# Sixteen of the thirty position bias thresholds as 0/1 tiles times a table on TensorE

## The reference, cut to what matters

```python
def _rel_bucket(rel):
    nb = REL_BUCKETS // 2
    max_exact = nb // 2
    n = jnp.abs(rel)
    large = max_exact + (jnp.log(jnp.maximum(n, 1).astype(jnp.float32) / max_exact)
                         / math.log(REL_MAX_DIST / max_exact) * (nb - max_exact)).astype(jnp.int32)
    large = jnp.minimum(large, nb - 1)
    return jnp.where(rel > 0, nb, 0) + jnp.where(n < max_exact, n, large)
...
        bucket = _rel_bucket(positions[:, None, :] - qpos[:, :, None])
        bias = jnp.moveaxis(rel_bias[bucket], -1, 1).astype(jnp.float32)
        s = jnp.where(key_chunk[None, :] <= qc[:, None], s + bias[:, :, None], -jnp.inf)
```

## Time and profile before

| | us |
|---|---|
| median of 3 runs | 2300.75 |
| lowest, highest | 2299.51, 2301.26 |
| the profiled execution | 2304.66 |
| its span in the profile | 2302.5 |
| PE busy in it | 2190.8 (95%) |
| DVE busy | 1599.7 (69%) |
| ACT busy | 1183.7 (51%) |

### The profile page before, as it was taken

One profiled execution on the slowest core, in us unless ns is written; L12 is line 12 of the kernel. 1 busy time (PEld: TensorE's weight loads), 2 busy tenths in 40 slices (PEclk: granted clock), 3 DMA queues, 4 the chain that ended last, 5 costly groups with the idle time before them and its releaser, 6 DMA issues.

```text
span 2302.5 us, 39325 instructions
## 1 busy us (share of the span) xinstructions
PE 2190.8 (95%) x17010; PEld 2056.2 (89%) x17010; DVE 1599.7 (69%) x2015; ACT 1183.7 (51%) x1405; POOL 0.2 (0%) x4
## 2 busy tenths in 40 slices
PE   6977999999899999999998999799999999998997
PEld 6856888888799999999998999799999999998997
DVE  8986899998696678446556665696676445657663
ACT  3534477777553554434854444353654436744442
POOL 0000000000000000000000000000000000000000
PEclk8978799999999999999999999899999999999999
DMA  8544399999544544444333444254544444344552
GB/s 343 193 172 150 149 374 373 371 369 364 201 166 161 184 151 166 147 147 149 109 134 140 165 173 173 112 182 148 186 165 165 152 159 148 110 150 144 186 189 83
DMA packets 64316, 432.06 MB, mean 188 GB/s; under 512 B 7792, under 2 KB 11152, under 8 KB 13712
## 3 DMA queue, kind: packets, MB, share of 16 engines
q1 hardware_dynamic: 64144, 429.56, 51.1%
HBM read 428.45 MB, written 1.08 MB: 187 GB/s over the span
## 4 chain that ended last, share of the span: by engine, by line
PE 88%; DVE 7%; ACT 2%; issue 1%; DMA 1%; SPq 0%; ACTq 0%; DVEq 0%
PE banks L1823 63%; PE banks L1841 10%; PE quad L1841 5%; DVE area_y L2295 1%; PE quad L552 1%; PE single L565 1%; DMA spare<-in_units_first 1%; PE quad L516 1%; PE quad L452 1%; DVE slot_rounded L998 1%; PE quad L555 1%; PE quad L500 1%; PE quad L540 1%; ACT area_y_rounded L650 0%; PE quad L472 0%
## 5 line engine op out<-in xcount | busy, mean ns | idle before, releaser
L1823 PE MATMUL banks<-spare_rounded,slot_rounded 128*128 128x272 f32 (+1 forms) x2176 | 624.8, 287 | 0.0
L1823 PE MATMUL banks<-spare_rounded,area_y_rounded 128*128 128x272 f32 (+1 forms) x1504 | 439.1, 292 | 15.1 <-DVE hn_rounded L987 13.1
L1823 PE MATMUL banks<-area_x_rounded,slot_rounded 128*128 128x272 f32 (+1 forms) x1568 | 447.0, 285 | 0.0
L1823 PE MATMUL banks<-hn_rounded,area_y_rounded 128*128 128x272 f32 (+1 forms) x1504 | 432.1, 287 | 0.0
L1823 PEld LDWEIGHTS banks<-spare_rounded,slot_rounded 128*128 128x128 f32 x2176 | 413.2, 190 | 0.0
L998 DVE TENSOR_TENSOR slot_rounded<-slot,area_y_rounded 128x2048 fp32r<-128x2048 f32 x118 | 269.6, 2289 | 161.2 <-ACT area_y_rounded L650 161.1
L1823 PEld LDWEIGHTS banks<-spare_rounded,area_y_rounded 128*128 128x128 f32 x1504 | 286.5, 190 | 17.5 <-DVE hn_rounded L987 14.0
L1823 PEld LDWEIGHTS banks<-area_x_rounded,slot_rounded 128*128 128x128 f32 x1568 | 297.2, 190 | 0.0
L1823 PEld LDWEIGHTS banks<-hn_rounded,area_y_rounded 128*128 128x128 f32 x1504 | 286.1, 190 | 0.1
L650 ACT ACTIVATE area_y_rounded<-slot 128x2048 fp32r<-128x2048 f32 x118 | 223.7, 1906 | 32.8 <-PE banks L1823 32.8
L998 DVE TENSOR_TENSOR slot_rounded<-slot,area_x_rounded 128x2048 fp32r<-128x2048 f32 x52 | 119.0, 2292 | 93.2 <-ACT area_x_rounded L650 93.1
(11 more groups left out here) (544 smaller groups left out, 5102.2 us busy)
## 6 DMA issues: line engine op xcount, KB each, us to landing
slot<-in_units_second SPq DMA_DIRECT2D x236, 1024.0 KB, 4.8
slot<-in_units_moe SPq DMA_DIRECT2D x100, 1024.0 KB, 5.1
slot<-in_units_first SPq DMA_DIRECT2D x32, 1024.0 KB, 5.6
spare<-in_units_moe SPq DMA_DIRECT2D x20, 1024.0 KB, 5.0
spare<-in_units_first SPq DMA_DIRECT2D x6, 1024.0 KB, 5.3
slot<-in_units_second SPq DMA_DIRECT2D x8, 768.0 KB, 4.2
merged<-acs_rows SPq DMA_DIRECT2D x4, 544.0 KB, 5.2
slot<-in_units_first SPq DMA_DIRECT2D x2, 576.0 KB, 4.0
```

The lines of the kernel that those rows point to most:

```text
L1823: ins = nc.tensor.matmul(out, weights[w], x[a], start=start and i == 0, stop=stop and i == 2, **kw)
```

## The change

The fourteen lowest thresholds stay as they were. For the other sixteen the distance of 256 keys to a query is compared on another layout: partition p = 16 g + r holds threshold r for the eight groups g of keys. `bias_key` is key position minus threshold, for 16 keys of each group of the first query block (128 keys) and 32 of the second's (256 keys), 48 in all. `reach_keys(part)` writes, for 16 of these, a tile [128, 16 keys, 128 queries] of ones where the key minus the threshold is at or above the query's position. `bias_table` [128, 32] holds in row p the four heads' steps of threshold r, in the four columns of group g, and zeros elsewhere. PE multiplies each [128, 128] tile with the table (48 matmuls of 32 columns in three parts of 16), which sums the thresholds and gives 128 queries by 8 groups by 4 heads. The three parts go to banks of `quad` at 1536, 0 and 512: the bank of x's mean square and those of the first two modulation pairs. They stand behind every second early unit. `bias_products` adds the results to `bias`. The mask addition moves from before the modulation pairs to before `weights_low(8)`.

The position input grows by 48 and the parameter input by 65 columns.

```diff
+BIAS_DIRECT = 14
+BIAS_GROUPS, BIAS_ROWS = 8, len(BUCKET_STARTS) - BIAS_DIRECT
+BIAS_KEYS = SCORES // BIAS_GROUPS
+BIAS_WIDTH = BIAS_GROUPS * DIFF_HEADS
...
+BIAS_BANKS = (1536, 0, 512)
...
     tick(ins, s.x_stat)
-    for u in ADA_EARLY:
+
+    def bias_keys(part):
+
+        pe.wait_ge(s.bias_reached.sem, s.bias_reached.at(0, part + 1))
+        if part == 0:
+            pe.wait_ge(s.x_root.sem, 1)
+        else:
+            pe.wait_ge(s.h1_ready.sem, part)
+        for n in range(16):
+            at = BIAS_BANKS[part] + BIAS_WIDTH * n
+            nc.tensor.matmul(m.quad[:, at:at + BIAS_WIDTH], m.bias_reach[:, 16 * part + n, :], m.bias_table, start=True, stop=True, skip_group_check=True)
+
+    for n, u in enumerate(ADA_EARLY):
         ada_rows(u)
+        if n % 2 and n < 6:
+            bias_keys(n // 2)
...
     link(copy(m.pos[:, :], m.pos_int[:, :]))
+    tick(tt(m.bias_table, p1("bias_of", 0, BIAS_WIDTH), p1("bias_before", 0, BIAS_WIDTH), ALU.subtract), s.dve1_step)
+    tick(ts(m.bias_key, m.pos[:, 2 + SEQ:], p1("bias_start"), None, ALU.subtract), s.dve1_step)
...
-    steps = list(range(len(BUCKET_STARTS)))
+    steps = list(range(BIAS_DIRECT))
+
+    def reach_keys(part):
+
+        keys, queries = slice(16 * part, 16 * part + 16), 2 + (128 if part else 0)
+        tick(tt(m.bias_reach[:, keys, :], m.bias_key[:, keys].unsqueeze(2).to_broadcast([128, 16, 128]),
+                m.pos[:, queries:queries + 128].unsqueeze(1).to_broadcast([128, 16, 128]), ALU.is_ge), s.bias_reached)
+
+    def bias_products():
+
+        for part, at in enumerate(BIAS_BANKS):
+            a, n, first_key = (0, 128, 0) if part == 0 else (128, 256, 16 * part - 16)
+            out = m.bias[:, :, a:a + n].rearrange("p h (g n) -> p h g n", g=BIAS_GROUPS)[:, :, :, first_key:first_key + 16]
+            products = m.quad[:, at:at + 512].rearrange("p (n g h) -> p h g n", g=BIAS_GROUPS, h=DIFF_HEADS)
+            tick(tt(out, products, out, ALU.add), s.dve1_step)
...
-    settle()
-    bias_steps(1)
-    v.wait_ge(m.loaded_early.sem, 16)
-    settle()
-    tick(tt(m.bias, m.bias, m.chunks.unsqueeze(1).to_broadcast([128, DIFF_HEADS, SCORES]), ALU.add), s.dve1_step)
+    for part in range(2):
+        reach_keys(part)
...
-        if pair < 2:
+        if pair == 0:
+            reach_keys(2)
+        elif pair == 1:
             bias_steps(1)
...
     weights_low(2)
-    bias_steps(2)
+    settle()
+    bias_products()
+    settle()
+    bias_steps(1)
     weights_low(3)
...
     normalise_rows(0, m.dq_tok)
     bias_steps(2)
+    settle()
+    tick(tt(m.bias, m.bias, m.chunks.unsqueeze(1).to_broadcast([128, DIFF_HEADS, SCORES]), ALU.add), s.dve1_step)
     weights_low(8)
...
     normalise_rows(2, m.q_tok)
-    bias_steps(1)
     root = roots(3)
...
             root.rearrange("p (b h) -> p b h", b=2).unsqueeze(3).to_broadcast([128, 2, MLA_HEADS, MLA_ROPE]), ALU.mult), s.rows_normed)
-    bias_steps(3)
     read_ada(8)
...
         normalise(i)
         if i in ADA_PAIR_BEHIND:
             read_ada(ADA_PAIR_BEHIND[i])
-        if i < 7:
-            bias_steps(2 if i in (2, 5) else 1)
-            settle()
```

More of the change, by code:

```diff
@@ L1393 @@
                  (6, 22), (7, 23), (8, 24), (12, 25), (16, 26), (23, 27), (32, 28), (46, 29), (64, 30), (91, 31)]
+BIAS_DIRECT = 14
+BIAS_GROUPS, BIAS_ROWS = 8, len(BUCKET_STARTS) - BIAS_DIRECT
+BIAS_KEYS = SCORES // BIAS_GROUPS
+BIAS_WIDTH = BIAS_GROUPS * DIFF_HEADS
+assert BIAS_GROUPS * BIAS_ROWS == 128
+BIAS_BANKS = (1536, 0, 512)
 TWO_PI = (6.28125, 0.0019350051879882812, 3.0199159819e-07)
@@ L1398 @@
                ("dq_g", 1), ("dk_g", 1), ("lambdas", 4), ("subln", 1), ("rel_bias", BUCKETS * DIFF_HEADS),
-               ("b_router", ROUTER), ("w_router", KT * ROUTER), ("c", KT), ("q_rope", MLA_ROPE), ("k_rope", MLA_ROPE), ("inv_freq", MLA_ROPE // 2)]
+               ("b_router", ROUTER), ("w_router", KT * ROUTER), ("c", KT), ("bias_start", 1), ("bias_of", BIAS_WIDTH), ("bias_before", BIAS_WIDTH), ("q_rope", MLA_ROPE), ("k_rope", MLA_ROPE), ("inv_freq", MLA_ROPE // 2)]
 PAR1_AT, PAR1 = {}, 0
@@ L2617, in first_signals @@
     s.lambda_products = Signal(sem("first_lambda_products"))
+    s.bias_reached = Signal(s.lambda_products.sem, 0, 1)
     s.lambda_sums = Signal(sem("first_lambda_sums"))
@@ L2789, in program @@
         a = Area(cpad)
-        m.par1, m.pos_int = a.cut(PAR1), a.cut(2 + SEQ).bitcast(I32)
+        m.par1, m.pos_int = a.cut(PAR1), a.cut(2 + SEQ + BIAS_KEYS).bitcast(I32)
+        m.bias_key, m.bias_table = a.cut(BIAS_KEYS), a.cut(BIAS_WIDTH)
+        a = Area(area_x)
+        a.at = 2048
+        m.bias_reach = a.cut(BIAS_KEYS, 128)
         a = Area(area_x)
@@ L2845, in program @@
         m.latent_sums, m.latent_roots, m.kpe_sums, m.out_sums, m.out_roots = a.cut(4), a.cut(4), a.cut(2), a.cut(8), a.cut(8)
-        m.steps, m.pos, m.mod, m.gain1 = a.cut(4 * len(BUCKET_STARTS)), a.cut(2 + SEQ), a.cut(48), a.cut(KT)
+        m.steps, m.pos, m.mod, m.gain1 = a.cut(4 * len(BUCKET_STARTS)), a.cut(2 + SEQ + BIAS_KEYS), a.cut(48), a.cut(KT)
         m.lam, m.silu_c, m.logits = a.cut(8), a.cut(KT), a.cut(2, ROUTER)
@@ L3114, in second_parameters, with bias_tables, bias_positions @@
     return np.stack(layers, axis=1)
+def bias_tables(rel_bias):
+    of, before = np.zeros((128, BIAS_WIDTH), np.float32), np.zeros((128, BIAS_WIDTH), np.float32)
+    for p in range(128):
+        g, row = p // BIAS_ROWS, BIAS_DIRECT + p % BIAS_ROWS
+        heads = slice(DIFF_HEADS * g, DIFF_HEADS * g + DIFF_HEADS)
+        of[p, heads], before[p, heads] = rel_bias[BUCKET_STARTS[row][1]], rel_bias[BUCKET_STARTS[row - 1][1]]
+    starts = np.tile(np.array([[start] for start, _ in BUCKET_STARTS[BIAS_DIRECT:]], np.float32), (BIAS_GROUPS, 1))
+    return {"bias_start": starts, "bias_of": of, "bias_before": before}
+def bias_positions(pos):
+    groups = np.concatenate([pos[0:128].reshape(BIAS_GROUPS, -1), pos.reshape(BIAS_GROUPS, -1)], axis=1)
+    return np.repeat(groups, BIAS_ROWS, axis=0)
 def first_parameters(i):
@@ L3129, in first_parameters @@
          "w_router": np.concatenate([i["w_rg"][0], i["w_re"][0]], axis=1).reshape(KT, 128, ROUTER).transpose(1, 0, 2).reshape(128, -1),
-         "c": columns_of(i["c"][0]), "inv_freq": row(freq)}
+         "c": columns_of(i["c"][0]), "inv_freq": row(freq), **bias_tables(np.asarray(i["rel_bias"]))}
     return packed(PAR1_FIELDS, PAR1_AT, PAR1, v)
@@ L3148 @@
         "in_slot_index": slot_numbers(),
-        "in_positions": np.concatenate([pos.reshape(2, 128).T, np.tile(pos[None, :], (128, 1))], axis=1),
+        "in_positions": np.concatenate([pos.reshape(2, 128).T, np.tile(pos[None, :], (128, 1)), bias_positions(pos)], axis=1),
         "in_x": by_features(i["x"][0]), "in_meta": by_features(i["meta_2"]),
```

## The result

| | median of the runs (lowest to highest) | profiled execution | its span |
|---|---|---|---|
| before | 2301.01 us (2299.51 to 2302.23, 4 runs) | 2304.66 us | 2302.5 us |
| changed | **2282.95 us** (2279.69 to 2283.43, 4 runs) | 2279.69 us | 2277.9 us |

The ratio is 0.9919, 95% interval 0.9902 to 0.9936: the changed kernel is faster, by 18.1 us between the medians and 18.6 us by the ratio, give or take 4. The forecast was 2283.0 us, range 2276 to 2293. The total came out as forecast; two of its terms did not, and their errors nearly cancel, so that the hit to 0.1 us is luck.

What follows compares the result with a forecast made beforehand. PE was taken as the main bound, with DVE's bias steps delaying it before 300 us. Terms 4.3 - 7.2 - 15.1 + 0.2 = -17.8 us, against the median of 2300.75, gave 2283.0 us, range 2276 to 2293.

Steps and rivals of the forecast that it cites:

- The reading of the stops: Early modulation units: PE's three "issue" stops are waits for its next 256 instructions, a block at most every 6.2 us.
- Term (a): Early modulation units on PE, 15.4 to 36.3 us: new matmuls and a fourth stop end them at 41.1, +4.8 us.
- the step "at full clock": Early units walked through at full clock, 3.4 us a new part, with four stops: they end 4.8 us later.
- Term (b): `w_in` units 0 to 6: DVE takes 34.0 us from last `h1_low` to unit 6's low part; +4.3 us left.
- Term (d): PE's wait for `k_read`: three bias steps leave its front on DVE, -7.2 us.
- Term (e): MLA head loop, first scores to turn of head 7: PE becomes the bound, 44.3 to 29.2 us, -15.1 us.
- the one head put at half clock: Head loop: of six heads, five at 3.23 us and one at half clock, 5.40 us; 21.6 us together.
- the first turn: Head loop: up to the turn of head 1, 9.26 us less 1.71 idle, 7.55 us.
- Rival 1: Early units: new records fall into idle time, costing 0.5 us instead of 4.3; total 2279.2 us; 12%.
- Rival 2: Head loop: PE stays at half clock in five of six heads, gain 6.5 us; total 2291.6 us; 15%.
- Rival 3: Early units and head loop: new parts bring half clock, first part 6.8 us; slower, 2306.4 us; 4%.
- Rival 4: Gain given back: products 1.5 us each (+2.4), +9 early, five heads at half clock; 2298.7 us, no change; 7%.

Runs made afterwards that it cites:

- e3: Kernel before plus 96 cheap unused matmul records (32 columns of weights, 64 of data) on PE at the three places of the new parts: 2308.06 us, ratio 1.0028.
- a1: The changed kernel run again, unedited: 2284.44 us, ratio 0.9928 to the kernel before.
- e4: Kernel before plus four unused fp32 matmuls of 512 columns at each of the three places, 24 records in all: 2300.25 us, ratio 0.9993.
- e1: Kernel before without the nine bias steps of the head loop: 2287.04 us, ratio 0.9932.
- e8: e7 with the first two parts moved ahead of x's mean square and the third behind the second pair of units: 2282.51 us, ratio 0.9918 to the kernel before.
- e9: Kernel before without the three bias steps ahead of `k_read`: 2293.77 us, ratio 0.9966.
- e10: Kernel before without the nine bias steps of the head loop and the three ahead of `k_read`: 2278.60 us, ratio 0.9898.
- e5: Kernel before without all sixteen bias steps and with nothing in their place: 2276.76 us, ratio 0.9896.
- e6: Changed kernel with the three products on DVE moved into its wait for the last modulation pair: 2281.39 us, ratio 0.9913 to the kernel before.
- e7: e6 with tiles and table in fp32r, one pass in place of two, 48 records for 96: 2275.97 us, ratio 0.9892 to the kernel before.
- e7b: e7 run again, unedited, beside a1: 2278.04 us, ratio 0.9900 to the kernel before.

## Why the prediction was right, and where it was off

**The reading of the stops held.** "I read the stops as PE waiting for its next block of 256 instructions": e3 shows all four stops of the count, a1 the fourth one in the changed kernel itself, the instruction queue has a packet 2.3 to 2.6 us ahead of the end of each, and e4 shows that as much time in few records moves next to nothing. "At most every 6.2 us" was too exact: the stops of e3 end 5.4 to 7.0 us apart. The sentence of the Trainium skill, "Runtime: NRT & Kernel Launch", section "Instruction fetch mechanics", that crossing a block is mostly hidden, is again not what these traces show: 12.5 us of PE idle at four crossings in e3, and 0.3 to 1.0 us at single ones in the head loop.

**Term (a) was mis-sized**: +4.8 forecast, +7.26 in the first profile, +6.9 in a1. 1.65 and 0.63 us of this are a later start of the units; all kernels of this study start them between 15.3 and 17.1 us, those with the old inputs too (e1 at 16.84; e8 apart), so most of it is likely scatter and not the 0.2 us of larger inputs. The rest is the length: 5.6 and 6.3 us more than before, where the step "at full clock" gave 4.8. That step failed in two ways. The price was too low: the first part ran at full clock and took 3.8 us, 0.117 a record from one start to the next, not 0.107. And the clock fell (0.50 from 23 to 26 us, from 31 to 32 and from 37 to 43): the last part took 5.73 us, and the second and the last pair 3.50 and 3.40, where 128 matmuls take 1.99 at full clock. Much of that time a stop for a block would have taken anyway, which is why the end stands only 0.8 to 1.5 us beyond the forecast length.

**Term (b) held**: 33.95 us against 34.0, products at 0.63 against 0.7. +6.65 of +7.26 were left, and +4.3 of +4.8 in the forecast.

**Term (d) held**: from the low part to the first scores -7.16 us in the first profile, -7.2 forecast; in e9 the first scores came 6.97 us earlier. In the changed kernel they came only 0.5 us early, not 2.7, because of term (a). In a1 they came 0.6 us late; its clock was 0.72 from 80 to 86 us, where that of the first profile was full.

**Term (e) was mis-sized the other way**: the loop took 25.72 us, which is where the bound "all at full clock, 25.7" lay, and not 29.2. The two steps that failed are the one head put at half clock and the first turn: "9.26 less 1.71 idle, 7.55" carried the half clock of the scores, which goes together with PE's 5.67 us wait for `k_read` (e1 keeps the wait and keeps the slow first heads; e9 and e10 have no wait there, and full clock in the first heads). To the turn of head 1 it took 6.16 us and then 3.16 to 3.76 a head. The longest of these is head 7, where a stop of 0.32 us stands. The gain was 18.55 us, not 15.1. Part of it is where the block ends happened to fall: the same loop has 1.4 to 1.9 us of stops in e1, e5 and e10.

The errors of (a), 2.4 us too little cost, and of (e), 3.4 us too little gain, nearly cancel, which is luck: -19.06 at turn 7 against -17.8, and -17.5 in a1.

**Profile and medians.** The profiled executions differ by 25.0 us, the medians by 18.1. The profiled execution of before lies 3.6 us above its median, that of the changed kernel 3.3 below. Behind turn 7 the shift grows from -19.1 to -21.7 us by 280 us and to -24.6 at the end. But e4, whose time is that of before, also stands 1.5 us ahead of before's profile at 280 us (0.5 at 213) and 2.6 at the end, and a1, the same kernel as the changed one, goes the other way, from -17.5 to -16.7 by 280 us. So these microseconds look like those of the single executions and not of the change; no run isolates them.

**The rivals.** Rival 1: above. Rival 2, half clock in the head loop, didn't come: 1.00 from 130 to 145 us with three transposes in every head. The section "Part 4: PE-mode transpose" of the Trainium skill's page "TensorE: Matmul & The Clock Gate", by which transposes don't count as busy for the clock in the same way, would have favoured this rival; no effect of it shows in these windows. Rival 3 named its sign, a first part of 6.8 us. The changed kernel's first part took 3.80. Such parts came in e6 (7.04 us, the second and third), the units took 30.6 us of the 33 it gave, and the time was still 20 us under before: what it lacked was the second half, the slow head loop. In e6 the clock was 0.50 early and 1.00 from 124 to 148 us, so the one doesn't bring the other. Rival 4 had one of its three pieces, the early one, at +7.3 of its +9.

**Left open.** Why PE falls to half clock in some executions of the same early work and not in others (second part 4.15, 4.37 and 7.04 us in the changed kernel, a1 and e6, whose PE work is the same). Why an instruction packet comes 39.8 us into one execution and 41.5 into another of the same kernel. And whether the stops would go if the data loads came earlier or later, which wasn't tried.

## What to carry to other kernels

Where a trace shows "issue" stops at even counts of instructions, look in the instruction queue for a packet ahead of each stop's end, and if there is one, price new work by its records first and by its time second: here 11 us of long matmuls cost nothing that the runs could tell, and 96 short records, 2 us of work at full clock, cost 6. Take the form with the fewest records (one pass in place of two here), and ask what stands on either side of the idle time that is filled. And where PE stops waiting, let one end of the range have its clock full behind the former wait: here a wait of 4.6 us cost its length and then some 2.5 us more in the work behind it.

## What the runs showed of the hardware that was not expected

- PE's granted clock was at half (0.50, 1.2 GHz) from 24 to 40 us in e6, while PE was never idle and issued matmuls of 32 and 64 columns; with matmuls of 512 columns in the same places (e4) it was 1.00 throughout. So a fall of the clock came without idle time before it.
- At half clock a record of the new products took 0.22 us (7.04 for 32), at full clock 0.12 (1.93 for 16 in e7), in fp32 and in fp32r alike (16 in 3.60 us at half clock in e7): so the cost goes by the number of passes, not by the type.
- PE waited for instruction blocks in the head loop too: 0.32 us in the changed kernel, 0.79 and 1.02 us in e5, these two 126 recorded matmuls apart. Each ended 2.3 to 2.4 us behind a packet of the instruction queue (144.0 in the changed kernel, 131.2 and 138.3 in e5).
- The price of a block end depends on the execution: at the same block end in the first `w_in` unit e7b stood still for 3.04 us and e7 for less than 0.2, which made 2.7 us at the first scores and 0.4 at 280 us.
